# Weight slots 64 bytes longer, one fixed order in the wide products, and another order of the first transfers

## What is computed

```python
x = x + mix                                    # first block, each layer
h = rmsnorm(x, norm_ffn[l])
x = x + (silu(h @ w_gate[l]) * (h @ w_up[l])) @ w_down[l]

x = layer_norm(alpha * x + 0.5 * swiglu_2(x, w_ff1_in[l], w_ff1_out[l]), ...)   # second block, each layer
x = layer_norm(alpha * x + hybrid_mixer(x, ...), ...)
x = layer_norm(alpha * x + 0.5 * swiglu_2(x, w_ff2_in[l], w_ff2_out[l]), ...)
```

## Time and profile before

| | |
|---|---|
| median of three runs | 2287.16 us |
| the profiled execution | 2286.68 us, of which the span from first to last instruction is 2284.9 us |
| TensorE (PE) busy | 2271.5 us, 99% of the span |
| VectorE (DVE) busy | 1783.0 us, 78% |
| ScalarE (ACT) busy | 1286.1 us, 56% |
| mean share of the 16 DMA engines | about a half, 179 GB/s read |
| mean granted TensorE clock | 0.999 of full speed |

### The profile page before, as it was taken

The page is one execution under the profiler, slowest core; times in us unless marked ns, Lnnn a source line. Parts: engine busy times, 40 slices in busy tenths (PEclk is TensorE's granted clock), DMA queues, the critical chain, the costliest instruction groups (busy, mean ns, idle before and its releaser), DMA issues.

```text
span 2284.9 us, 37627 instructions
## 1 busy us (share of the span) xinstructions
PE 2271.5 (99%) x15111; PEld 2058.5 (90%) x15111; DVE 1783.0 (78%) x2713; ACT 1286.1 (56%) x2016; POOL 79.6 (3%) x96
## 2 busy tenths in 40 slices
PE   9999999999999999999999999999999999999998
PEld 8988889998888888999999888988889999998887
DVE  7898658879758876897679886698767976798854
ACT  7855455655445544585666554465545856565542
POOL 0022000002100000020000000000000200000000
PEclk9999999999999999999999999999999999999999
DMA  6466565446556566554455555566665543556563
GB/s 242 138 196 191 189 209 175 150 157 220 176 183 212 191 189 193 200 176 130 132 174 193 192 192 188 165 201 203 189 191 200 175 138 121 183 181 217 187 184 100
DMA packets 115084, 412.45 MB, mean 181 GB/s; under 512 B 12896, under 2 KB 14304, under 8 KB 114656
## 3 DMA queue, kind: packets, MB, share of 16 engines
q1 hardware_dynamic: 114336, 406.91, 55.6%
q0 software_dynamic: 288, 2.10, 0.3%
q10 hardware_dynamic: 288, 1.05, 0.1%
HBM read 408.96 MB, written 1.05 MB: 179 GB/s over the span
## 4 chain that ended last, share of the span: by engine, by line
PE 88%; DVE 8%; ACT 2%; issue 1%; DMA 0%; SPq 0%; POOL 0%; DVEq 0%; ACTq 0%
PE ps L452 87%; DVE wlo L2012 3%; DVE region L2804 1%; ACT whi L1250 1%; ACT region L1472 1%; DMA raw<-in_ew_c 0%; PE ps L721 0%; DVE region L2331 0%; DVE RX L2201 0%; DVE x L2059 0%; DVE region L2334 0%; DVE x L2208 0%; DVE region L2447 0%; DVE region L2474 0%; DVE region L2973 0%
## 5 line engine op out<-in xcount | busy, mean ns | idle before, releaser
L452 PE MATMUL ps<-xx,whi 128*128 128x512 f32 (+1 forms) x4504 | 1202.9, 353 | 3.7 <-DVE xx L2067 2.4
L2012 DVE TENSOR_TENSOR wlo<-raw,whi 128x1024 fp32r<-128x1024 f32 (+3 forms) x772 | 925.5, 1207 | 273.3 <-ACT whi L1250 272.2
L1250 ACT ACTIVATE whi<-raw 128x1024 fp32r<-128x1024 f32 (+3 forms) x772 | 801.1, 1043 | 517.5 <-PE ps L452 506.8
L452 PEld LDWEIGHTS ps<-xx,wlo 128*128 128x128 f32 x3696 | 694.2, 188 | 118.7 <-DVE wlo L2012 0.2
L452 PE MATMUL ps<-xx,wlo 128*128 128x256 f32 x3696 | 796.8, 279 | 0.0
L452 PEld LDWEIGHTS ps<-xx,whi 128*128 128x128 f32 x4504 | 690.8, 188 | 9.1 <-issue 3.2
L452 PE MATMUL ps<-H,whi 128*128 128x512 f32 (+1 forms) x2144 | 539.0, 339 | 0.1
L452 PE MATMUL ps<-H,wlo 128*128 128x256 f32 x1632 | 364.0, 279 | 0.0
L452 PEld LDWEIGHTS ps<-H,wlo 128*128 128x128 f32 x1632 | 306.4, 188 | 46.8
L452 PEld LDWEIGHTS ps<-H,whi 128*128 128x128 f32 x2144 | 329.6, 188 | 1.6 <-issue 0.6
L2007 DVE TENSOR_REDUCE t<-ps 128x256 f32<-128x512 f32 x320 | 219.7, 688 | 41.1 <-PE ps L452 37.0
(11 more groups left out here) (316 smaller groups left out, 1592.5 us busy)
## 6 DMA issues: line engine op xcount, KB each, us to landing
raw<-in_sg SPq DMA_DIRECT2D x128, 512.0 KB, 4.2
raw<-in_su SPq DMA_DIRECT2D x128, 512.0 KB, 4.2
raw<-in_sd SPq DMA_DIRECT2D x128, 512.0 KB, 4.1
raw<-in_mw_g SPq DMA_DIRECT2D x48, 512.0 KB, 3.7
raw<-in_fg SPq DMA_DIRECT2D x44, 512.0 KB, 3.3
raw<-in_fu SPq DMA_DIRECT2D x44, 512.0 KB, 3.3
raw<-in_fd SPq DMA_DIRECT2D x32, 512.0 KB, 3.5
raw<-in_mw_a SPq DMA_DIRECT2D x24, 512.0 KB, 4.1
```

Source lines behind the costliest of these rows:

```text
L452: return e.matmul(out, lhsT, rhs, start=start, stop=stop, skip_group_check=True)
L1250: e.activation(m.whi[:, c % NHL, 0:cw], m.raw[:, c % NRAW, 0:cw], ACT.Copy).then_inc(s["whi"].h, s["whi"].up(c))
L2012: e.tensor_tensor(m.wlo[:, c % NHL, 0:cw], m.raw[:, c % NRAW, 0:cw], m.whi[:, c % NHL, 0:cw].bitcast(F32), ALU.subtract).then_inc(s["wlo"] ...
```

## The change

Four things change. The rows of a slot of `whi` and `wlo` become 64 bytes longer, so successive slots begin 64 bytes apart when counted past a multiple of 512, and the gaps are chosen anew: `raw` follows without a gap, `whi` begins 128 past a multiple of 512, `wlo` 448, `x` 256, `xx`, `t12` and the region with `H` 320. `mm2` loses its `turn`: always high, then low. `WARM` goes from 14 to 18. The two halves of x are brought by SP's queue behind the first weights, and `pk` by ScalarE's.

```diff
-WARM = 14
+WARM = 18
@@ lay_memory
-    line(0)
     m.raw = sb("raw", [128, NRAW, CW])
-    line(0)
-    m.whi = sb("whi", [128, NHL, CW], F32R)
-    line(0)
-    m.wlo = sb("wlo", [128, NHL, CW], F32R)
-    line(0)
+    line(128)
+    m.whi = sb("whi", [128, NHL, CW + 16], F32R)
+    line(448)
+    m.wlo = sb("wlo", [128, NHL, CW + 16], F32R)
+    line(256)
     m.x = sb("x", [128, 8, 256])
-    line(64)
+    line(320)
     m.xx = sb("xx", [128, 8, 2, 256], F32R)
-    at = line(64)
+    at = line(320)
     t12 = sb("t12", [128, 2048 + 128])
...
-    at = line(64)
+    at = line(320)
     left = nc.sbuf_bytes_remaining
-    nar = min((left() if callable(left) else left) // 4 - 8 - 4096, 21696)
+    nar = min((left() if callable(left) else left) // 4 - 4096, 21696)
@@ tensor_program
-    turn = [0]
-
     def mm2(b, wh, wl, a, start):
 
-        turn[0] ^= 1
-        if turn[0]:
-            mm(b[:, :], wh, a.rearrange("p a b -> p (a b)"), start=start, stop=False)
-            return mm(b[:, 0:256], wl, a[:, 0, :], start=False, stop=True)
-        mm(b[:, 0:256], wl, a[:, 0, :], start=start, stop=False)
-        return mm(b[:, :], wh, a.rearrange("p a b -> p (a b)"), start=False, stop=True)
+        mm(b[:, :], wh, a.rearrange("p a b -> p (a b)"), start=start, stop=False)
+        return mm(b[:, 0:256], wl, a[:, 0, :], start=False, stop=True)
@@ scalar_program
-    for p in range(2):
-        e.dma_start(m.x[:, 4 * p:4 * p + 4, :], ins["x"][:, 4 * p:4 * p + 4, :]).then_inc(
-            s[f"x{p}"].h, s[f"x{p}"].up("in", by=16))
+    e.dma_start(m.pk[:, :], ins["pack"]).then_inc(s["pk"].h, s["pk"].up("in", by=16))
@@ sync_program, constants
         if c == 1:
-            load("pk", "in", m.pk[:, :], ins["pack"])
+            for p in range(2):
+                load(f"x{p}", "in", m.x[:, 4 * p:4 * p + 4, :], ins["x"][:, 4 * p:4 * p + 4, :])
```

## The result

The changed kernel took 2294.48 us (median of 7 runs, 2294.33 to 2294.58) beside 2287.07 us of the kernel before (7 runs on the same chip): a ratio of 1.0032, 95% interval 1.0021 to 1.0044. It is slower by 7.4 us, where 2274.1 was forecast.

What follows compares the result with a forecast made beforehand. The prediction took TensorE as the bound, busy 2271.5 of 2284.9 us. From 2286.7 us it took 12.6 for the distances (-6.7 wide pairs, -5.9 triples) and 0 for the rest: 2274.1 us, range 2254 to 2311.

Steps and rivals of the forecast that it cites:

- Distances: Bytes, modulo 512, from weight slots to moving operands: five instead of one free some chunks of stalls, together -12.6 us.
- Order: Products always high, low, high, low: price inside the bounds of -37.7 and +31.6 us, given nothing of its own.
- The lever: TensorE's 4000 wide pairs (high product of 512 columns, low of 256): one ns in the pair is 4 us.
- the lower bound: No stall left: wide pair 340 ns instead of 345.0, -20.0 us; with the narrow products, together -37.7 us.
- I take one third of the stalls as gone: Some chunks settle in the good state, others not: -6.7 us for wide pairs, -5.9 for narrow products.
- the triples: 1320 narrow groups on TensorE (high, low, high, 256 columns each) at 353.4 ns: near 349 on the mean, -5.9 us.
- The argument behind it: At one distance nothing ends a state, good or bad; five distances give each chunk of 16 or 24 products a new start.
- Rival (a): The old distance of 64 was the good one: wide pairs up to +5.0 ns, +23.6 us, 2310; chance 0.35.
- Rival (b): Distances don't act, timing alone settles a state: 0 and the front's bounds, 2286.7 us; chance 0.12 with small remainders.
- the longer rows and the moved raw: Weight rows 64 bytes longer, raw off a multiple of 512: ScalarE and VectorE queue as before, nothing.
- the front: Start with moved transfers and more warm-up: first product may come earlier, sum of squares still ends at 19.4 us; 0 (+0.4 to -1.5).
- the two signs that were to prove me wrong: Chunk pace follows its distance and most are above 345 ns; or pace follows the order alone, whatever the slot.

Runs made afterwards that it cites:

- 64 and 256: High loads 64, low loads 256 bytes from the moving operand, modulo 512; for all slots, order high, low, high, low, against the kernel before: 2267.12 us.
- 64 and 64: High and low loads both 64 bytes from the moving operand, as in the kernel before; with only the order changed to high, low, high, low: 2311.81 us.
- 320 and 256: High loads 320, low loads 256 bytes from the moving operand for all slots, order high, low, high, low, against the kernel before: ratio 0.9930.
- 64 and 192: High loads 64, low loads 192 bytes from the moving operand for all slots, order high, low, high, low, against the kernel before: 2294.76 us.

## Why the prediction was wrong

**The failed step is "Distances", and with it "Order".** The two terms can't be measured apart: alone they are +17 and +25 us, together +7.4. The lever was right (4 us for each ns of the pair), and so was the lower bound: a pair without a stall is 340 ns, now seen over nearly all 4000 pairs in one kernel. What failed in "Distances" is "I take one third of the stalls as gone": it takes some slots as freed and the others as left near the 345 ns of before. In fact slot 2 alone went down by 5 ns, and slots 0, 1, 3 and 4 went up by 2 to 5: 350 and 347 where the chunks had 345.0. The forecast's 343.3 became 347.0, its -6.7 us became +7.8, and the triples' -5.9 became +2.0.

**The argument behind it was turned the wrong way.** It said that at one distance a state, good or bad, has nothing to end it, and that a new start for each chunk would help. The first half is what the runs show: 521 pairs kept 350 ns, and nearly 4000 kept 340. But that speaks for one distance, in the good pace, and not for five. Five distances give each chunk a new entry, and the next chunk pays what the one before left: with one and the same 64 and 256 a slot ran at 340.2 in the changed kernel and at 349.0 behind other distances.

**The order "nothing of its own"** was wrong in size and in kind. At the old distances it costs 25 us by itself (351.4 ns a pair), so the kernel that the five distances were to improve was not the one of the earlier trace rows. Against that base the spread layout is a gain of 17 us, 351.4 to 347.0; I had it measured from 345.0. Its price lay within the bounds of 340 and 352 for the pair, near their upper end, and I gave it nothing, with no row for it. The earlier trace rows pointed the right way: seven pairs in the new order at 350 ns.

**Rival (a)** has the right side and the right point of decision (the mean pair above 345.0), at a third of its price; that the measured time lies in the stated range is owed to this rival, which the range took in. Its reason, that 64 bytes was the good distance, is refuted for the new order: there 64 and 64 is 351.4 ns, slower than the mean of the changed kernel, and the best slot is one with another low distance, at 340 and not at the 345 that the rival allowed it. In the old order the reason stands as far as it was tested: 64 and 64 has 345.0 ns, the five other pairs of distances 347.8 to 350.2. **Rival (b)**, that distances don't act, is refuted by 2267.1 against 2311.8 us with the same instructions in the same order.

The Trainium skill, "TensorE: Matmul & The Clock Gate", section "Step-by-step: what each phase is for", has two independent read ports, so that loading the next weights takes nothing from the running matmul. By that rule, as the prediction took it, no distance matters, and these two kernels disagree: 340.1 against 351.4 ns a pair with only the addresses of weights and moving operands changed; the measurement decides. Whether it is the loads that hold up the products, no run shows.

**Right:** the longer rows and the moved raw cost ScalarE and VectorE nothing (busy 1286.1 and 1783.8 us against 1286.1 and 1783.0); the front is 0, with its mechanism: the first product came before 8.99 us, the gap in the clock was closed, and the chain fourth weights, squares, sum ended 0.15 us earlier and no more. Of the two signs that were to prove me wrong, the first came: most chunks above 345, with a pace that follows the distance, though not the distance alone.

**What stays open.** Why 64 and 256, and 320 and 256, fit this order, and why the alternating order fits 64 and 64 better, was not settled; no run shows what the two readers do in each other's way, or whether the distance to the moving operand counts or that of high weights to low ones, since both change together. That distances count modulo 256 rather than 512 is suggested by pairs of values that agree (low 128 and 384: 347.3 and 346.7 ns; high 64 and 320 at low 256: 340.1 both; 64 and 320 at low 320: 352.7 and 353.9), not tested by itself; one pair of values speaks against it (high 64 and 320 at low 192: 346.9 and 352.3), unless these are the two paces, 346.7 and 353.3, that 64 and 192 has by itself. A layout with all triples at 340 ns as well, nearly 18 us more (1320 x 13.4 ns), was not found.

## What to carry to other kernels

Where TensorE is full and streams long runs of one pattern, read the pace start to start and not the busy sums: two ns in a pair that occurs 4000 times are 8 us. Try the order of the products and the places of weights and moving operands together, since each alone can lose what both together win, and give all weight slots the same distance once a pair of distances runs free, so that a chunk hands its good pace to the next. Then look at several runs: a pace with a slower neighbour can be lost at one late product and kept for hundreds.

## What the runs showed of the hardware that was not expected

- The time of a high and a low product with the next weights' loads under them depends on addresses: from 340.1 ns (64 and 256 in the order high, low, high, low) to 353.9 ns (320 and 320), 4%, with no wait or idle time in the rows.
- One arrangement has several steady paces. 64 and 256: 340 and 350 ns. 64 and 64: 349 and 353.4. 64 and 192: 346.7 and 353.3, and 340 and 356.6 for its triples. A pace lasted up to 1111 pairs (388 us) with nothing between; other work between two pairs sometimes changed it (one product of 256 columns, 348.9 to 353.4 ns) and sometimes not (two such products, 350 before and after).
- The order by itself turns good into bad: at 64 and 256, 340.1 ns in one order and 350.0 in the other; at 64 and 64, 351.4 and 345.0.
- The granted clock between 8.5 and 13.3 us was 1.00 of 2.4 GHz instead of 0.64 when eight more warm-up passes left only 0.94 us idle ahead of the first product instead of 2.43, and that was worth nothing to the whole, since weights and statistics came only 0.15 us earlier.
